# Experts' gate and up products in three fp32r passes for six of eight k-tiles, and expert weights read in whole rows per partition

## The chip, the cores and the metric

The kernel runs on one core of a Trainium2 chip. The metric is the device time of one execution in microseconds (us). Its engines: TensorE (PE), VectorE (DVE), ScalarE (ACT), GpSimd (POOL), and SyncE (SP), which issues most DMAs. 16 DMA engines move the data.

## What is computed

A two-layer decoder trunk for 512 prompt tokens and 64 sample tokens (576 rows of width 1024). Each layer is a mixer (layer 0: gated DeltaNet and pooling; layer 1: RG-LRU), a LayerNorm, a mixture of 16 experts, and a LayerNorm. The change is in the experts:

```python
    y = jnp.zeros_like(xt)
    for e in range(N_EXPERTS):
        h = jax.nn.silu(xt @ w_gate[e]) * (xt @ w_up[e])
        y = y + combine[:, e:e + 1] * (h @ w_down[e])
```

`w_gate[e]` and `w_up[e]` are 1024 x 512, `w_down[e]` is 512 x 1024, all float32: 2 MB each. Each token uses two of the 16 experts.

## The kernel before

Tokens are sorted on the chip into one block of up to 128 slots per expert. Per expert `g` (0 to 15 in layer 0, 16 to 31 in layer 1) the work is:

- POOL gathers the expert's rows of x by an indirect DMA into `XG[u]` (`u = g % 2`; weights and rows have two buffers each).
- PE transposes them in eight 128 x 128 pieces (`gather_transposed`), and DVE copies these out of PSUM into `XGT` (`x_copied`, L1985 and L1986). The eight pieces are the eight k-tiles of the contraction over 1024.
- PE multiplies `XGT` with the gate weights (`gate`, L1001) and the up weights (`up`, L1008) in plain float32. Each k-tile of 128 x 512 is one `matmul` in the source, and two MATMUL instructions in the trace.
- ACT makes the silu (L1384), DVE multiplies it with the up product (L1992), PE transposes the result (L1015), and ACT copies it out twice: rounded to fp32r as `HT_HIGH`, and in full as `HT`.
- `down` (L1026) multiplies it with the down weights in three fp32r passes: high x high, high x low, low x high. ACT makes `WDN_HIGH` by rounding, four copies of 128 x 1024; DVE subtracts that from the weights to make `WDN_LOW` (L2006), and the same for `HT_LOW` (L2005).
- ACT and DVE copy the result out (halves of `YO`), and ACT issues its store to `y_rows` (L1392).

The order on each engine is written out by hand. PE's step for expert g is `gate(g)`, `h_transposed(g-1)`, `up(g)`, `gather_transposed(g+1)`, `down(g-1)`. The last expert of a layer has its own `last_down`, plain float32 (L1037).

SP issues the weight loads in a fixed order, two experts ahead, each when its buffer has been read: after gate(g) the gate weights of g+2 (L431), after up(g) the up weights of g+2 (L434), after down(g) the down weights of g+2 (L437). As down(g-1) comes after gate(g) and up(g) on PE, and its load before theirs on SP, the three issues come together at the end of each step:

```python
                    for u in range(2):
                        sp.wait_ge(gate_ps, i * 2 + (base + u + 1))
                        sp.dma_start(WGT[u], moe_w_gate[l, bass.ds(i * 2 + (2 + u), 1)]
                                     .rearrange("o (k p) f -> p (o k) f", p=P)).then_inc(gate_in[u], 16)
                        sp.wait_ge(up_ps, i * 2 + (base + u + 1))
                        ...
                        sp.wait_ge(y0_ps, i * 2 + (base + u + 1))
```

## Time and profile before

| | |
|---|---|
| time, median of 3 runs | 1580.51 us (1578.92 to 1580.55) |
| profiled execution | 1581.12 us, of it 1578.8 us span |
| PE busy | 1350.4 us, 86% of the span |
| DVE, ACT, POOL busy | 693.1, 425.1, 208.6 us |
| mean granted PE clock | 0.903 of full speed |
| moved by DMA | 296.52 MB, mean 188 GB/s |

The rows that follow are of this one profiled execution; its time outside the span is 2.3 us. PE's busy time is modelled at a matmul's end, so that neighbouring matmuls overlap: the distance from start to start is the cost of one in a stream. The experts of layer 0 run from about 504 to 845 us, those of layer 1 from about 1190 to 1525 us.

### The profile page before, as it was taken

How to read it: one execution, taken by the hardware profiler on the slowest of the kernel's cores; microseconds unless marked ns; L12 is line 12 of the kernel's file. 1: busy time of each engine (PE TensorE's matmuls, PEld its weight loads, DVE VectorE, ACT ScalarE, POOL GpSimd, SP SyncE). 2: the span in 40 equal slices, each digit the busy share in tenths (PEclk: the TensorE clock that was granted, in tenths of full speed). 3: DMA queues.
4: the chain of work that ended last, by engine and by line, in shares of the span. 5: the costliest groups of instructions: out<-in, count | busy, mean ns of one | idle time of the engine just before them, and what ended most of it. 6: DMA issues, size and time to landing. Idle time of an engine off the chain costs nothing. (4 is left out here: it accounts for less than half of the span.)

```text
span 1578.8 us, 15547 instructions
## 1 busy us (share of the span) xinstructions
PE 1350.4 (86%) x5941; PEld 907.8 (57%) x5941; DVE 693.1 (44%) x1192; ACT 425.1 (27%) x667; POOL 208.6 (13%) x272
## 2 busy tenths in 40 slices
PE   5999878888995999999993289978959999999950
PEld 4989877854444555555551289843454555555530
DVE  2765345524244234443332823656442334333328
ACT  2533222220010222223332332262111333332213
POOL 3102142202000000000002200153001000000013
PEclk9999889995995999999996589998969999999985
DMA  6120140010616499999974511103264999999933
GB/s 182 54 81 28 54 146 1 1 48 11 216 72 226 166 363 354 368 361 357 357 267 149 188 54 54 69 39 110 80 232 147 331 358 357 355 356 357 329 118 118
DMA packets 132695, 296.52 MB, mean 188 GB/s; under 512 B 6608, under 2 KB 32937, under 8 KB 132640
## 3 DMA queue, kind: packets, MB, share of 16 engines
q1 hardware_dynamic: 120736, 252.77, 45.4%
q0 software_dynamic: 7296, 26.22, 4.7%
q10 hardware_dynamic: 4608, 16.78, 2.6%
q8 instruction: 37, 0.61, 0.2%
q14 instruction: 18, 0.15, 0.0%
HBM read 268.86 MB, written 26.89 MB: 187 GB/s over the span
## 5 line engine op out<-in xcount | busy, mean ns | idle before, releaser
L1001 PE MATMUL bank<-work 128*128 128x512 f32 x512 | 229.3, 601 | 5.5 <-DVE work L1986 5.5
L2006 DVE TENSOR_TENSOR WDN_LOW<-work,WDN_HIGH 128x1024 fp32r<-128x1024 f32 x120 | 141.4, 1220 | 201.6 <-ACT WDN_HIGH L1155 201.6
L1008 PE MATMUL bank<-work 128*128 128x512 f32 x512 | 225.0, 592 | 0.0
L1155 ACT ACTIVATE work<-bank 128x512 f32<-128x512 f32 (+4 forms) x180 | 79.4, 477 | 495.1 <-PE bank L1026 361.0
L1001 PEld LDWEIGHTS bank<-work 128*128 128x128 f32 x512 | 98.3, 193 | 118.6 <-issue 109.7
L1008 PEld LDWEIGHTS bank<-work 128*128 128x128 f32 x512 | 94.9, 190 | 108.1 <-issue 108.1
L1155 ACT ACTIVATE WDN_HIGH<-work 128x1024 fp32r<-128x1024 f32 x120 | 116.8, 1044 | 18.4 <-ACT work L1155 18.4
L1026 PE MATMUL bank<-WDN_HIGH,HT_HIGH 128*128 128x512 f32 x240 | 96.9, 404 | 0.0
L1026 PE MATMUL bank<-WDN_HIGH,HT_LOW 128*128 128x512 f32 x240 | 93.7, 390 | 0.0
L1026 PE MATMUL bank<-WDN_LOW,HT_HIGH 128*128 128x512 f32 x240 | 93.3, 389 | 0.0
L2301 POOL COPY idx_cur<-idx_all 128x1 int32 (+1 forms) x32 | 5.9, 185 | 657.4 <-PE bank L993 465.6
L927 PE MATMUL bank<-work,XT 128*128 128x512 f32 (+1 forms) x192 | 83.2, 593 | 0.0
L1155 ACT ACTIVATE W_HIGH<-work 128x1024 fp32r<-128x1024 f32 x36 | 38.0, 1058 | 150.8 <-PE bank L590 80.6
L1992 DVE TENSOR_TENSOR work<-work,bank 128x512 f32<-128x512 f32 x32 | 22.0, 688 | 114.3 <-PE bank L1008 114.3
L914 PE MATMUL bank<-work,XT 128*128 128x512 f32 x128 | 62.4, 652 | 5.6 <-POOL XT L2362 4.5
L927 PEld LDWEIGHTS bank<-work,XT 128*128 128x128 f32 (+1 forms) x192 | 32.9, 172 | 48.5 <-issue 48.5
L576 PE MATMUL bank<-ident,X 128*128 128x128 f32 (+1 forms) x120 | 18.6, 323 | 48.0 <-POOL X L2294 36.7
L1569 DVE SCALAR_TENSOR_TENSOR work<-work,par 128x512 f32<-128x512 f32 x120 | 56.9, 516 | 2.1
L1384 ACT ACTIVATE work<-bank 128x512 f32<-128x512 f32 x32 | 19.1, 597 | 136.8 <-PE bank L1001 136.8
L1330 ACT ACTIVATE lnw<-lnw 128x1 f32<-128x1 f32 (+1 forms) x20 | 4.1, 203 | 189.9 <-DVE lnw L1846 189.9
L1997 DVE COPY work<-bank 128x512 f32<-128x512 f32 x32 | 22.1, 692 | 66.2 <-PE bank L1026 46.2
L1026 PEld LDWEIGHTS bank<-WDN_HIGH,HT_LOW 128*128 128x128 f32 x240 | 45.0, 188 | 9.8
(438 smaller groups left out, 2537.1 us busy)
## 6 DMA issues: line engine op xcount, KB each, us to landing
work<-in_moe_w_gate_dram SPq DMA_DIRECT2D x32, 2048.0 KB, 14.6
work<-in_moe_w_up_dram SPq DMA_DIRECT2D x32, 2048.0 KB, 19.5
work<-in_moe_w_down_dram SPq DMA_DIRECT2D x32, 2048.0 KB, 9.9
y_rows<-work ACTq DMA_DIRECT2D x32, 512.0 KB, 8.3
work<-in_ab_w_in_dram SPq DMA_DIRECT2D x10, 1024.0 KB, 5.3
work<-in_c_w_in_dram SPq DMA_DIRECT2D x8, 1024.0 KB, 8.5
x_rows<-X SPq DMA_DIRECT2D x8, 512.0 KB, 2.6
work<-in_c_w_out_dram SPq DMA_DIRECT2D x1, 4096.0 KB, 12.7
```

The source lines that it names most:

```text
L576: last = tr(heads_of(b + k // 4, P, r)[:, k % 4, :], rows[0:r, t, P * k:P * k + P], ident[0:r, 0:r])
L914: last = mm(bank[2 * (t % 2) + half][0:ROWS[t], :], XT[:, k, tile_cols(t)], (WO_A, WO_B)[l][k][:, 512 * half:512 * half + 512], start=(k = ...
L927: last = mm(bank[2 * (t % 2) + half][0:ROWS[t], :], XT[:, k, tile_cols(t)], (WO_A, WO_B)[l][k][:, 512 * half:512 * half + 512], start=(k = ...
L1001: last = mm(bank[u][:, :], XGT[:, k, :], WGT[u][:, k, :], start=(k == 0), stop=(k == KD - 1))
L1008: last = mm(bank[2 + u][:, :], XGT[:, k, :], WUP[u][:, k, :], start=(k == 0), stop=(k == KD - 1))
L1026: last = mm(bank[7 - half][:, :], x[:, f, :], w[:, f, cols], start=(f == n == 0), stop=(f == 3 and n == 2))
L1155: return nc.scalar.activation(out, in_, ACT.Copy, scale=scale)
L1384: nc.scalar.activation(SG[u], bank[u][:, :], ACT.Silu).then_inc(sg_done, 1)
L1569: last = V.scalar_tensor_tensor(dst, src, w, dst, ALU.mult, ALU.add)
L1992: V.tensor_tensor(HB[u], SG[u], bank[2 + u][:, :], ALU.mult).then_inc(h_ready, 1)
L1997: V.tensor_copy(YO[u][:, 512:1024], bank[6][:, :]).then_inc(y1_out, 1)
L2006: last = V.tensor_tensor(WDN_LOW[u][:, f, :], WDN[u][:, f, :], WDN_HIGH[:, f, :].bitcast(F32), ALU.subtract)
```

## The change

1. Gate and up: of each weight's eight k-tiles, the first six are multiplied in three fp32r passes as `down` is, the last two stay plain float32. A unit is two k-tiles. ACT rounds a unit (a copy of 128 x 1024) into one of four `GU_HIGH` buffers, DVE subtracts it in place from the weights, and PE gives the `GU_HIGH` buffer back after its six matmuls (`gu_used`).
2. The transposed rows of x are no longer copied by DVE but rounded by ACT (three copies) and split by DVE (two subtractions). The transposed product is split straight from PSUM, so `HT` is gone.
3. `WDN_HIGH` is rounded, split and given back in four parts (`down_used`), and `down` runs over parts outside and halves inside. `last_down` is gone: the last expert is done as the others are.
4. The weights lie in SBUF as `(p k)` and not `(k p)`: a partition gets eight (or four) neighbouring rows of the matrix, 16 KB in one piece, where it had eight pieces of 2 KB (gate, up) or four of 4 KB (down). To fit, the transposes take every eighth (fourth) column (`every`).
5. Some semaphores outside the experts are shared under new numbers, and the overflow path (taken only if an expert has more than 128 tokens) follows the new layout.

```diff
             def gate(l, e, u):
-                sp.dma_start(WGT[u], moe_w_gate[l, e].rearrange("(k p) f -> p k f", p=P)).then_inc(gate_in[u], 16)
+                sp.dma_start(WGT[u], moe_w_gate[l, e].rearrange("(p k) f -> p k f", p=P)).then_inc(gate_in[u], 16)
...
-                    last = tr(heads_of(4 + k // 4)[:, k % 4, :], XG[u][:, P * k:P * k + P], ident[:, :])
+                    last = tr(heads_of(4 + k // 4)[:, k % 4, :], every(XG[u], KD, k), ident[:, :])
                 last.then_inc(xg_ps, 1)
 
+            def unit(psum, unit_no, slot_no_, n, low):
+
+                pe.wait_ge(gu_split, unit_no + 1)
+                for k in range(2 * n, 2 * n + 2):
+                    x_low = XGT_LOW_A[:, k, :] if k < 4 else XGT_LOW_B[:, k - 4, :]
+                    w_high = GU_HIGH[slot_no_][:, k % 2, :]
+                    for m, (x, w) in enumerate(((XGT_HIGH[:, k, :], w_high), (XGT_HIGH[:, k, :], low[:, k, :]), (x_low, w_high))):
+                        last = mm(psum, x, w, start=(k == m == 0), stop=(k == KD - 1 and m == 2))
+                last.then_inc(gu_used, 1)
...
+                for n in range(UNITS):
+                    unit(bank[u][:, :], 2 * UNITS * g + n, (2 * UNITS * u + n) % 4, n, WGT_LOW[u])
                 pe.wait_ge(gate_in[u], arrivals(l, pairs))
-                at_least(pe, sg_done, g - 1)
-                for k in range(KD):
-                    last = mm(bank[u][:, :], XGT[:, k, :], WGT[u][:, k, :], start=(k == 0), stop=(k == KD - 1))
-                last.then_inc(gate_ps, 1)
+                plain(bank[u][:, :], WGT[u]).then_inc(gate_ps, 1)
...
+                def round_units(which, pairs, u, g):
+
+                    w, arrived, first = (WGT, gate_in, 0) if which == "gate" else (WUP, up_in, UNITS)
+                    act.wait_ge(arrived[u], arrivals(l, pairs))
+                    for n in range(UNITS):
+                        at_least(act, gu_used, 2 * UNITS * g + (first + n - 3))
+                        copy(GU_HIGH[(2 * UNITS * u + first + n) % 4][:, :, :], w[u][:, 2 * n:2 * n + 2, :]).then_inc(gu_rounded, 1)
...
-                def step(i, v):
+                def step(i, v, more=True):
 
                     u, g = (1 + v) % 2, i * 2 + (base + 1 + v)
+                    round_units("up", i + (v + 1), u, g)
+                    h_rounded(g - 1)
                     silu(u, g)
-                    h_copied(g - 1)
+                    if more:
+                        round_units("gate", i + 2, 1 - u, g + 1)
+                        x_rounded(g + 1)
+                    round_down(i + (v + 1), u, g)
                     result(i + 1, 1 - u, g - 1, i * 2 + v)
-                    round_down(i + (v + 1), u, g)
...
                     u, g = (1 + v) % 2, i * 2 + (base + 1 + v)
+                    split_units("up", u, g)
+                    h_split(g - 1)
+                    if more:
+                        split_units("gate", 1 - u, g + 1, range(UNITS - 1))
                     h_product(u, g)
-                    x_copied(g + 1)
+                    if more:
+                        split_units("gate", 1 - u, g + 1, range(UNITS - 1, UNITS))
+                        x_split(g + 1)
+                    split_down(u, g)
                     result(i + 1, 1 - u, g - 1)
-                    split_down(u, g)
```

PE at the gate product of one expert and what follows it, before (`bank<-work` at L1001 is gate, at L1008 up, L1015 the transposes of h):

```order
L1001 MATMUL bank<-work 128x512 [waits sg_done,gate_in0,xgt_ready]
L1001 MATMUL bank<-work 128x512 x7
L1015 MATMUL bank<-ident,work 128x128 [waits y0_out,h_ready]
L1015 MATMUL bank<-ident,work 128x128 x3
L1008 MATMUL bank<-work 128x512 [waits h_ready,up_in0]
L1008 MATMUL bank<-work 128x512 x7
```

and PE of the changed kernel from the sixth k-tile of a gate product to the first matmul of the up product (L1021 is `plain`, L1043 the transposes of h):

```order
L1015 MATMUL bank<-GU_HIGH_49,XGT_HIGH 128x512
L1015 MATMUL bank<-WGT_LOW_54,XGT_HIGH 128x512
L1015 MATMUL bank<-GU_HIGH_49,XGT_LOW_B 128x512
L1021 MATMUL bank<-work 128x512 [waits gate_in1]
L1021 MATMUL bank<-work 128x512
L1043 MATMUL bank<-ident,work 128x128 [waits h_ready]
L1043 MATMUL bank<-ident,work 128x128 x3
L1015 MATMUL bank<-GU_HIGH_50,XGT_HIGH 128x512 [waits gu_split]
```

Six k-tiles have become three matmuls each; where PE waited once for a weight's load, it now waits for DVE's split of each unit.

ACT from one silu to the next step, before (`work<-bank` at L1155 is a copy of `HT`, then of the result; L1392 the store):

```order
L1384 ACTIVATE work<-bank 128x512 [waits gate_ps]
L1155 ACTIVATE HT_HIGH<-bank 128x512 [waits h_ps]
L1155 ACTIVATE work<-bank 128x512
L1155 ACTIVATE work<-bank 128x512 [waits y0_ps]
L1392 DMA y_rows<-work 128x1024 [waits y1_out,y0_out]
L1155 ACTIVATE WDN_HIGH<-work 128x1024 [waits y0_ps,down_in1]
L1155 ACTIVATE WDN_HIGH<-work 128x1024 x3
```

and the same stretch of ACT in the changed kernel (L1414 silu, L1422 the store, the last row the next step's first up unit):

```order
L1414 ACTIVATE work<-bank 128x512 [waits gate_ps]
L1173 ACTIVATE GU_HIGH_49<-work 128x1024 [waits gu_used,gate_in0]
L1173 ACTIVATE GU_HIGH_50<-work 128x1024 [waits gu_used]
L1173 ACTIVATE GU_HIGH_51<-work 128x1024 [waits gu_used]
L1173 ACTIVATE XGT_HIGH<-bank 128x512 [waits xg_ps]
L1173 ACTIVATE XGT_HIGH<-bank 128x256
L1173 ACTIVATE work<-bank 128x256
L1173 ACTIVATE WDN_HIGH<-work 128x1024 [waits down_used,down_in1]
L1173 ACTIVATE WDN_HIGH<-work 128x1024 [waits down_used] x3
L1173 ACTIVATE work<-bank 128x512 [waits down_used]
L1422 DMA y_rows<-work 128x1024 [waits y1_out,y0_out]
L1173 ACTIVATE GU_HIGH_52<-work 128x1024 [waits gu_used,up_in0]
```

Between silu and the rounding of the down weights, ACT now has the gate units of the next expert, which wait for their load, and the copies of x; the store has moved behind the rounding of the down weights, and the up units behind the store.

DVE over the same stretch in the changed kernel (L2047 splits of units, L2030 the product h, L2022 and L2023 the splits of x, L2054 those of the down weights, L2039 the copy of the result):

```order
L2047 TENSOR_TENSOR WGT_LOW_53<-work,GU_HIGH_49 128x1024 [waits gu_rounded]
L2047 TENSOR_TENSOR WGT_LOW_53<-work,GU_HIGH_50 128x1024 [waits gu_rounded]
L2030 TENSOR_TENSOR work<-work,bank 128x512 [waits sg_done,up_ps]
L2047 TENSOR_TENSOR WGT_LOW_53<-work,GU_HIGH_51 128x1024 [waits gu_rounded]
L2022 TENSOR_TENSOR XGT_LOW_A<-bank,XGT_HIGH 128x512 [waits xgt_high]
L2023 TENSOR_TENSOR XGT_LOW_B<-bank,XGT_HIGH 128x256
L2054 TENSOR_TENSOR WDN_LOW_64<-work,WDN_HIGH 128x1024 [waits down_rounded] x4
L2039 COPY work<-bank 128x512 [waits down_used]
L2047 TENSOR_TENSOR WUP_LOW_55<-work,GU_HIGH_52 128x1024 [waits gu_rounded]
```

The two gate units, the product, the third unit, x, the four down parts, the result's copy and the first up unit now stand in one row on DVE; before, the product was followed by two copies of x, the result's copy and the down splits alone.

## Rows read from the trace of the kernel before

**Rows 1.** The page's slices of the span, and its DMA queues (packets, MB, share)

```profile
DMA  6120140010616499999974511103264999999933
GB/s 182 54 81 28 54 146 1 1 48 11 216 72 226 166 363 354 368 361 357 357 267 149 188 54 54 69 39 110 80 232 147 331 358 357 355 356 357 329 118 118
...
q1 hardware_dynamic: 120736, 252.77, 45.4%
...
q8 instruction: 37, 0.61, 0.2%
```

**Rows 2.** Windows: busy us and instructions per engine, granted clock, DMA share, GB/s

```profile
680.00:720.00 40.00, 40.00 (x135) 23.13 (x134) 14.96 (x18) 12.13 (x16) 2.31 (x4) 1.00 0.99 355
```

**Rows 3.** Timeline of PE over one expert's step: start, us, line, instruction

```profile
562.04 0.39 PE L1026 MATMUL bank<-WDN_LOW,HT_HIGH 128*128 128x512 f32 x1
...
567.05 0.39 PE L1026 MATMUL bank<-WDN_HIGH,HT_LOW 128*128 128x512 f32 x1
567.28 7.03 PE L1001 MATMUL bank<-work 128*128 128x512 f32 x16
574.14 0.60 PE L1015 MATMUL bank<-ident,work 128*128 128x128 f32 x4
574.58 7.03 PE L1008 MATMUL bank<-work 128*128 128x512 f32 x16
581.45 1.04 PE L993 MATMUL bank<-ident,work 128*128 128x128 f32 x8
582.24 0.47 PE L1026 MATMUL bank<-WDN_HIGH,HT_HIGH 128*128 128x512 f32 x1
...
587.79 7.03 PE L1001 MATMUL bank<-work 128*128 128x512 f32 x16
```

**Rows 4.** Timeline of SP's issues, and the DMA view's median us to landing

```profile
567.47 0.37 SPq L437 DMA_DIRECT2D work<-in_moe_w_down_dram  x1
568.43 0.38 SPq L431 DMA_DIRECT2D work<-in_moe_w_gate_dram  x1
...
work<-in_moe_w_gate_dram SPq DMA_DIRECT2D x32, 2048.0 KB, 14.6
```

**Rows 5.** Windows within that step

```profile
568.50:583.00 14.50, 14.50 (x45) 7.29 (x44) 6.49 (x7) 5.47 (x7) 0.18 (x1) 1.00 0.99 362
571.00:572.00 1.00, 1.00 (x4) 0.38 (x2) 0.00 (x0) 1.00 (x2) 0.00 (x0) 1.00 1.01 315
575.00:576.00 1.00, 1.00 (x4) 0.51 (x3) 0.05 (x1) 0.92 (x2) 0.00 (x0) 1.00 1.02 418
579.00:580.00 1.00, 1.00 (x4) 0.45 (x3) 0.00 (x0) 0.00 (x0) 0.00 (x0) 1.00 1.05 393
```

**Rows 6.** Groups by form, 526 to 793 us: busy us, mean ns, idle before

```profile
L1155 ACT ACTIVATE WDN_HIGH<-work 128x1024 fp32r<-128x1024 f32 x48 | 46.7, 1044 | 7.7 <-ACT work L1155 7.7
...
L1997 DVE COPY work<-bank 128x512 f32<-128x512 f32 x13 | 9.0, 692 | 19.5 <-PE bank L1026 19.5
```

**Rows 7.** Timeline of DVE and ACT in that step

```profile
576.56 2.35 DVE L2006 TENSOR_TENSOR WDN_LOW<-work,WDN_HIGH 128x1024 fp32r<-128x1024 f32 x2
...
568.11 0.34 ACTq L1392 DMA_DIRECT2D y_rows<-work  x1
568.55 3.90 ACT L1155 ACTIVATE WDN_HIGH<-work 128x1024 fp32r<-128x1024 f32 x4 [0.47 <-ACT work L1155]
574.84 0.59 ACT L1155 ACTIVATE HT_HIGH<-bank 128x512 fp32r<-128x512 f32 x1
```

**Rows 8.** Timeline of PE at the start and the end of layer 0's experts

```profile
526.14 7.13 PE L1001 MATMUL bank<-work 128*128 128x512 f32 x16 [1.38 <-DVE work L1986]
...
834.02 0.63 PE L1015 MATMUL bank<-ident,work 128*128 128x128 f32 x4 [0.78 <-ACT work L1155]
835.83 8.83 PE L1037 MATMUL bank<-work 128*128 128x512 f32 x16 [1.18 <-ACT work L1155]
```

**Rows 9.** Window in the last down product

```profile
838.00:840.00 2.00, 2.00 (x4) 0.83 (x3) 0.00 (x0) 0.00 (x0) 0.00 (x0) 0.50 0.00 0
```

More of the change, by code:

```diff
@@ L46 @@
 WORK = 35340
+UNITS = 3
 class Steps:
@@ L377, in samples, with every @@
             return ap[:, TP:T].rearrange("p (s l) -> p s l", s=NS)
+        def every(rows, n, k):
+            return rows.rearrange("p (c n) -> p n c", n=n)[:, k, :]
         def at_least(engine, s, value):
@@ L996, in gate, with plain @@
+            def plain(psum, w):
+                for k in range(2 * UNITS, KD):
+                    last = mm(psum, XGT[:, k, :], w[:, k, :], start=False, stop=(k == KD - 1))
+                return last
             def gate(l, pairs, u, g):
-                pe.wait_ge(xgt_ready, g * 2 + 2)
+                pe.wait_ge(xgt_ready, g + 1)
+                at_least(pe, sg_done, g - 1)
+                for n in range(UNITS):
+                    unit(bank[u][:, :], 2 * UNITS * g + n, (2 * UNITS * u + n) % 4, n, WGT_LOW[u])
@@ L1005, in up @@
                 pe.wait_ge(up_in[u], arrivals(l, pairs))
-                at_least(pe, h_ready, g - 1)
-                for k in range(KD):
-                    last = mm(bank[2 + u][:, :], XGT[:, k, :], WUP[u][:, k, :], start=(k == 0), stop=(k == KD - 1))
-                last.then_inc(up_ps, 1)
+                plain(bank[2 + u][:, :], WUP[u]).then_inc(up_ps, 1)
             def h_transposed(u, g):
@@ L1014, in h_transposed @@
                 for f in range(4):
-                    last = tr(heads_of(7)[:, f, :], HB[u][:, P * f:P * f + P], ident[:, :])
+                    last = tr(heads_of(7)[:, f, :], every(HB[u], FF // P, f), ident[:, :])
                 last.then_inc(h_ps, 1)
             def down(l, u, g):
-                pe.wait_ge(down_split, g + (1 - l))
+                pe.wait_ge(ht_ready, g + 1)
                 at_least(pe, y1_out, g)
-                for half, done in ((1, y1_ps), (0, y0_ps)):
-                    cols = slice(512 * half, 512 * half + 512)
-                    for f in range(4):
+                for f in range(4):
+                    pe.wait_ge(down_split, 4 * g + (f + 1))
+                    for half in (1, 0):
+                        cols = slice(512 * half, 512 * half + 512)
                         for n, (x, w) in enumerate(((HT_HIGH, WDN_HIGH), (HT_HIGH, WDN_LOW[u]), (HT_LOW, WDN_HIGH))):
@@ L1027, in down @@
                                       start=(f == n == 0), stop=(f == 3 and n == 2))
[L1028 to L1039 removed]
+                    last.then_inc(down_used, 1)
             def experts(l):
@@ L1083, in overflow @@
                             for k in range(KD):
-                                last = tr(heads_of(4 + k // 4)[:, k % 4, :], XG[0][:, P * k:P * k + P], ident[:, :])
+                                last = tr(heads_of(4 + k // 4)[:, k % 4, :], every(XG[0], KD, k), ident[:, :])
                             last.then_inc(s["pe"], 1)
@@ L1094, in overflow @@
                             for f in range(4):
-                                last = tr(heads_of(7)[:, f, :], HB[0][:, P * f:P * f + P], ident[:, :])
+                                last = tr(heads_of(7)[:, f, :], every(HB[0], FF // P, f), ident[:, :])
                             last.then_inc(s["pe"], 1)
@@ L1409, in experts @@
                     step(i, 1)
-                silu(1, base + 15)
-                h_copied(base + 14)
-                result(8, 0, base + 14, 14)
-                h_copied(base + 15)
+                step(NE // 2 - 1, 0, False)
+                h_rounded(base + 15)
                 result(8, 1, base + 15, 15)
@@ L1997, in result, with split_units @@
                     V.tensor_copy(YO[u][:, 512:1024], bank[6][:, :]).then_inc(y1_out, 1)
+                def split_units(which, u, g, some=range(UNITS)):
+                    w, low, first = (WGT, WGT_LOW, 0) if which == "gate" else (WUP, WUP_LOW, UNITS)
+                    for n in some:
+                        dve.wait_ge(gu_rounded, 2 * UNITS * g + (first + n + 1))
+                        high = GU_HIGH[(2 * UNITS * u + first + n) % 4][:, :, :].bitcast(F32)
+                        V.tensor_tensor(low[u][:, 2 * n:2 * n + 2, :], w[u][:, 2 * n:2 * n + 2, :], high, ALU.subtract)\
+                            .then_inc(gu_split, 1)
@@ L2008, in split_down, with step @@
-                    last.then_inc(down_split, 1)
-                def step(i, v):
+                        dve.wait_ge(down_rounded, 4 * g + (f + 1))
+                        V.tensor_tensor(WDN_LOW[u][:, f, :], WDN[u][:, f, :], WDN_HIGH[:, f, :].bitcast(F32),
+                                        ALU.subtract).then_inc(down_split, 1)
+                def step(i, v, more=True):
                     u, g = (1 + v) % 2, i * 2 + (base + 1 + v)
+                    split_units("up", u, g)
+                    h_split(g - 1)
+                    if more:
+                        split_units("gate", 1 - u, g + 1, range(UNITS - 1))
@@ L2026, in experts @@
                     step(i, 1)
-                h_product(1, base + 15)
-                result(8, 0, base + 14)
+                step(NE // 2 - 1, 0, False)
+                h_split(base + 15)
                 result(8, 1, base + 15)
```

172 lines of the change are left out of this document (91 added, 81 removed).

## The prediction

> **What bounds the kernel now.** I read the slices of the span first. In the two experts' stages DMA stands at 9 and near 355 GB/s [rows 1]. A window of 40 us inside shows both sides full: PE busy for all 40.00 us at granted clock 1.00, DMA share 0.99 [rows 2]. Which of the two sets the pace is read from the timeline of PE: one expert takes 587.79 - 567.28 = 20.51 us, and no row of it has a wait in front [rows 3]. So PE is the bound, and DMA has almost nothing to spare: about 7.3 MB per expert (three weights of 2.10 MB, a gather and a store of 0.52 MB each) in 20.51 us is 356 GB/s. DVE and ACT are busy 14.96 and 12.13 us of 40 [rows 2].
>
> The margin of the loads matters now. All three of a step are issued together when down ends at 567.3: down at 567.47, gate at 568.43, up behind [rows 4]. The gate load lands 14.6 us later, at 583.0, which is G = 15.7 us after the end of down. Today PE wants it at 587.8, so 4.8 us are spare.
>
> **What PE saves.** Plain float32: L1001 to L1015 is 6.86 us for 16 instructions, 0.429 each, 0.858 per k-tile [rows 3]. Three passes: from 562.04 to 567.28 are 23 starts of L1026, 0.228 each, 0.683 per k-tile [rows 3]. The saving is 0.175 us on each of 12 k-tiles per expert, 2.1 us. PE alone would need 18.4 us per expert. Over 32 experts that is 67 us, if nothing else waits: 1581 - 67 = 1514.
>
> **What ACT and DVE get.** ACT gets six copies of 128 x 1024 per expert at 1.044 us [rows 6] (0.95 apart in a row, 3.90 us for four [rows 7]), and the copies of x; it had 6.2 us of work per expert (12.13 x 20.51/40) and gets about 13. DVE gets six subtractions at 1.18 (2.35 us for two [rows 7]), 7.1 us on top of 7.7, about 15. Both fit in 18.4, so neither is a bound by its sum. The order is what costs.
>
> **The chain that I expect to set the pace.** The gate load of expert k+2 is still issued only when down(k-1) has ended. PE wanted it one whole step later; ACT now wants it in the middle of the step, right behind silu, to round its units, and ACT is in order: behind that wait stand the copies of x, the four parts of the down weights, the result's copy, its store, and the next up units. On DVE nearly all of these stand in one row too. From the landing of the gate weights:
>
> - ACT rounds the first unit: 1.04
> - DVE splits two units, 2.35; product h, 0.65; third unit, 1.2
> - DVE splits x: 0.69 for 512 columns as L1997 [rows 6], and 0.35 by size for 256; 1.05
> - DVE splits four down parts, 2 x 2.35 = 4.7, and copies the result, 0.69
> - ACT issues the store it held back for that copy, 0.34 [rows 7] and 0.1 for the handover
> - ACT rounds the first up unit, 1.04; DVE splits it, 1.2
>
> Together 14.4 us; then PE can start up(k+2). From there PE needs up (18 x 0.228 + 4 x 0.429 = 5.8), the transposes (0.79 from 581.45 to 582.24) and down (5.55 to 587.79) [rows 3], 12.2 us, until down(k+1) ends, which is two steps after the end of down(k-1). So two experts take G + 14.4 + 12.2 = G + 26.6 us, or twice 18.4 if that is more. Today two take 41.0. The change gains only while G is under 14.4, or a little above with the edges below.
>
> **G after the change.** Transfers start 1.2 us after down ends (568.5 [rows 5]). Ahead of the gate weights' last byte go down, gate, the store and some of up, which ran beside: by the window 362 GB/s x 14.5 us = 5.25 MB [rows 5]. Whole rows do not occur in the trace. Bounds for their pace: the same 362 GB/s from below; from above 418, the best microsecond, when 4 KB pieces of down and the store ran together [rows 5]. Pieces of 2 KB ran at 393 and the start of down at 315 [rows 5]. I take 400, nearer the upper row, because fewer and longer pieces lose less between them, and because the slow start is of one kind of piece only. With queued whole loads less of up should run ahead; I count half, 4.98 MB. G = 1.2 + 4.98/0.400 = 13.6. The bounds are 12.5 (4.72 MB at 418) and 15.7.
>
> Two experts then take 13.6 + 26.6 = 40.2, so 20.1 per expert against 20.51: a gain of 0.4. PE would wait 3.4 us in every second step, mostly in front of up.
>
> **The transfer page.** A rule of the Trainium skill speaks against even that: HBM Reference, section Specifications (TRN2), gives about 358 GB/s as the effective bandwidth per core, though it adds that a core streaming alone measures well above. The trace's 355 GB/s over 40 us looks like that figure; its 393 and 418 in single microseconds do not. By 358, G would be 1.2 + 4.98/0.358 = 15.1, two experts 41.7, and the sum 1584 in place of 1565. A pace capped like that is the slower rival below, which is worked out from the rows alone.
>
> **The sum.** Per layer: the first step after the preloaded experts has its weights and gains the full 2.1. Some 13 steps gain 0.4 each, 5.3. Gate and up of the first expert gain 2.1, but x now goes through ACT and then DVE in both transposes that PE waits for (today 1.38 us of waiting [rows 8]; then 0.59 + 0.6 on ACT [rows 7] and 1.05 on DVE, 0.9 more each), so 0.3 is left. The last down: 24 x 0.228 = 5.5 for 16 x 0.429 = 6.9, less 1.2 because the result's copy before it stands behind the rounding of the last down part and h is split after it is rounded; 0.2. Together 7.9 per layer, 15.8 for two. Profiled time 1581.1 less 15.8 is 1565.3; the median is 0.6 below the profiled execution, so 1565.
>
> Costed at nothing: `down` by parts (same 24 matmuls); the last two k-tiles' wait for the load (landed before its units were rounded); the routing ahead of the experts, where ACT and DVE round and split the first units while the gather is under way (without that cover three splits more, 3.5 us per layer); the semaphores elsewhere. Transposes of every eighth column appear in no row: nothing from below, and from above as much again as today's 0.79 and 0.44, which on the two-step chain is 0.8 to 1.2 per two experts, 11 to 16 us in all. I take nothing, as the same 12 pieces go through PE.
>
> **Rivals.**
>
> - *The loads come in time, and PE sets the pace.* For it: PE has no other wait, and 418 GB/s exists. If the store does not run ahead of the gate weights, G = 1.2 + 4.2/0.418 = 11.2, two experts 37.8, 18.9 each: 13 x 1.6 + 2.6 = 23 per layer, 1581 - 47 = 1534. The end of this case is 1514. Against it: G would have to fall by 4 us. Chance 0.18 (1512 to 1550).
> - *No change.* At about 366 GB/s G is 14.8 and the slower steps eat the 2.6 at the edges: 1578 to 1584. For it: the long window at 362. Chance 0.12.
> - *Slower: whole rows run at the same pace, and ACT wants them earlier.* G stays 15.7, two experts take 42.3, 21.15 each, 0.64 more: 13 x 0.64 - 2.6 = 5.7 per layer, 1592. It decides from 366 GB/s down. For it: 362 over 14.5 us. A sign that long pieces may even be slow: queue q8 moved 0.61 MB in 37 pieces of 16 KB in 0.2% of 16 engines' span, 50 us, 12 GB/s per engine, while q1 moved 252.77 MB in 45.4%, 22 GB/s [rows 1]; but single pieces for another destination don't tell of a stream. At 12 GB/s per engine G would be 27 and the time about 1740. Chance 0.16.
> - *Slower: PE's clock.* Before the last down PE waits 0.78 and 1.18 us, and its 16 instructions take 8.83 us in place of 7.03 [rows 8] with a stretch at granted clock 0.50, the 1.2 GHz level [rows 9]. After 1.38 us of waiting only 0.1 was lost [rows 8]. If every wait of 3.4 us brings 1.8 us of that, 13 times, 23 us go, and 1565 becomes 1588. Against it: the waits come after full work and partly split in two. Chance 0.10.
> - *Forecast:* 1550 to 1577, 0.44.
>
> **Range and chances.** 1565. From 1538 to 1592 I leave out the best end and the slowest loads, about 2 in 10. A measurement of this kernel tells about 0.2%, 3.2 us. Faster is 0.44 + 0.18 = 0.62, the same 0.12, slower 0.26.
>
> **What the changed profile would show.** The gate and up passes 0.228 us apart; steps that alternate or lie near 20 us; waits of PE in front of the units for DVE's splits and of ACT for the gate load; gate landing near 12.5 us after issue; a DMA rate near 400 in the burst; DVE without a gap from the third unit to the up unit. I am wrong if PE has no waits (the loads land by 11 us), if the whole rows run at 362 or less, if the granted clock falls in the loop, or if the transposes' instructions are longer.

## The result, and the profile after

The changed kernel took 1591.07 us (median of 5, 1587.50 to 1592.16) beside 1580.55 for the kernel before (5, 1578.92 to 1581.03): ratio 1.0064, 95% interval 1.0049 to 1.0079. It is slower by some 10 us; forecast was a gain of 15. The profiled execution took 1592.14 us, of it 1590.4 span, 11.6 more than before. The page of the changed kernel:

```profile
PE 1309.9 (82%) x6341; PEld 1002.1 (63%) x6341; DVE 909.5 (57%) x1394; ACT 636.9 (40%) x931; POOL 224.8 (14%) x272
...
DMA packets 63068, 296.58 MB, mean 186 GB/s; under 512 B 6608, under 2 KB 32937, under 8 KB 50720
...
PE 56%; DVE 17%; DMA 14%; issue 5%; ACT 4%; POOL 1%; ACTq 0%; SPq 0%; POOLq 0%; DVEq 0%
DMA work<-in_moe_w_gate_dram 12%; PE bank L1015 8%; PE bank L1055 6%; PE bank L939 5%; PE bank L601 4%; PE bank L602 4%; PE bank L629 3%; PE bank L630 3%; PE bank L926 3%; PE bank L1021 3%; DVE WDN_LOW L2054 2%; ACT GU_HIGH L1173 2%; PE bank L1148 2%; PE bank L950 1%; DVE X L1875 1%
...
L1173 ACT ACTIVATE GU_HIGH<-work 128x1024 fp32r<-128x1024 f32 x192 | 189.9, 1050 | 219.6 <-DMA work<-in_moe_w_gate_dram 117.3
...
work<-in_moe_w_gate_dram SPq DMA_DIRECT2D x32, 2048.0 KB, 13.3
work<-in_moe_w_up_dram SPq DMA_DIRECT2D x32, 2048.0 KB, 17.8
work<-in_moe_w_down_dram SPq DMA_DIRECT2D x32, 2048.0 KB, 8.0
```

PE is busy 40 us less than before, and the kernel is 12 us longer. The chain that ended last now holds the gate load with 12%, and in front of its units ACT waited 117 us for that load. It lands 13.3 us after its issue, 14.6 before [rows 4].

SP's issues of the down loads mark the ends of PE's steps. Before, all were 20.5 us apart. After, in layer 0, they are 18.5, 23.1, 18.5, 22.8, 19.1, 23.1, 19.6, 23.0, 18.5, 22.7, 18.7, 22.4 and 18.5: the alternation of two that was forecast, with a pair at 41.6 us on average (41.5 in layer 1), where 40.2 was forecast and 41.0 stood before. One pair (one of the longer, 42.2 us), in the timelines of SP, ACT, DVE and PE; in brackets what ended a wait:

```profile
631.08 0.33 SPq L449 DMA_DIRECT2D work<-in_moe_w_down_dram  x1
631.60 0.49 SPq L443 DMA_DIRECT2D work<-in_moe_w_gate_dram  x1
...
673.27 0.33 SPq L449 DMA_DIRECT2D work<-in_moe_w_down_dram  x1
...
646.15 2.96 ACT L1173 ACTIVATE GU_HIGH<-work 128x1024 fp32r<-128x1024 f32 x3 [6.92 <-DMA work<-in_moe_w_gate_dram]
...
657.62 0.34 ACTq L1422 DMA_DIRECT2D y_rows<-work  x1
658.42 2.96 ACT L1173 ACTIVATE GU_HIGH<-work 128x1024 fp32r<-128x1024 f32 x3 [4.02 <-PE bank L1015]
...
647.25 2.36 DVE L2047 TENSOR_TENSOR WGT_LOW<-work,GU_HIGH 128x1024 fp32r<-128x1024 f32 x2 [6.75 <-ACT GU_HIGH L1173]
...
652.19 4.62 DVE L2054 TENSOR_TENSOR WDN_LOW<-work,WDN_HIGH 128x1024 fp32r<-128x1024 f32 x4
656.72 0.69 DVE L2039 COPY work<-bank 128x512 f32<-128x512 f32 x1
659.51 3.50 DVE L2047 TENSOR_TENSOR WUP_LOW<-work,GU_HIGH 128x1024 fp32r<-128x1024 f32 x3 [2.10 <-ACT GU_HIGH L1173]
...
652.42 0.79 PE L1015 MATMUL bank<-GU_HIGH,XGT_HIGH 128*128 128x512 f32 x1 [2.30 <-DVE XGT_LOW_B L2023]
...
660.78 0.50 PE L1015 MATMUL bank<-GU_HIGH,XGT_HIGH 128*128 128x512 f32 x1 [0.31 <-DVE WUP_LOW L2047]
```

Down ended at 630.9, and ACT has the gate weights at 646.15: G = 15.3. From there DVE has no gap until it copies the result; PE starts up at 660.78, 14.6 us after the landing, and the next but one down ends 12.3 us later. (ACT's wait at 658.42 is put down to PE, but the store ahead of it on ACT had waited for DVE's copy.) The same stretches in windows (columns as in [rows 2]):

```profile
632.10:646.10 14.00, 13.64 (x59) 10.00 (x58) 6.64 (x7) 4.45 (x7) 0.45 (x2) 1.00 0.99 387
640.00:642.00 2.00, 2.00 (x11) 1.65 (x10) 0.49 (x1) 0.00 (x0) 0.00 (x0) 1.00 1.06 446
...
652.00:655.00 3.00, 2.58 (x6) 2.10 (x7) 3.00 (x4) 2.40 (x4) 0.00 (x0) 0.53 0.88 344
680.00:720.00 40.00, 37.20 (x153) 28.48 (x154) 28.00 (x30) 23.45 (x32) 4.19 (x4) 0.96 0.85 335
```

The burst moved at 387 GB/s, 5.42 MB before the gate weights' last byte. After its wait of 2.30 us PE ran at granted clock 0.53, near the 1.2 GHz level. In this pair that lies beside DVE's chain: PE still reached up 0.31 us before the split was ready (660.78). It is not so in every pair. The up product of 701.83 starts after a wait of 1.79 us for its split, and eight of its matmuls then start 0.42 us apart with nothing of DVE's left beside them: down ends 13.9 us after the start of up in place of 12.3. That is a pair of 42.7 us. In 40 us PE stands still for 2.8, and DMA's share is 0.85 where it was 0.99.

The rest of the loss is outside the steps. The timelines of POOL before and after, where a layer's first rows are fetched (first the kernel before, then the changed one):

```profile
498.65 0.19 POOL L2301 COPY idx_cur<-idx_all 128x1 int32<-128x1 int32 x1 [102.02 <-DVE idx_all L1978]
499.89 1.08 POOL L2303 DMA_INDIRECT work<-x_rows,idx_cur  x1 [1.05 <-issue]
```

```profile
498.53 1.02 POOL L2358 COPY idx_cur<-idx_all 128x1 int32<-128x1 int32 x1 [102.03 <-DVE idx_all L2015]
500.60 2.12 POOL L2360 DMA_INDIRECT work<-x_rows,idx_cur  x1 [1.05 <-issue]
...
498.29 3.49 DVE L2047 TENSOR_TENSOR WGT_LOW<-work,GU_HIGH 128x1024 fp32r<-128x1024 f32 x3
...
505.96 1.95 PE L1005 MATMUL bank<-ident,work 128*128 128x128 f32 x8 [7.80 <-DMA work<-x_rows,idx_cur]
510.20 0.79 PE L1015 MATMUL bank<-GU_HIGH,XGT_HIGH 128*128 128x512 f32 x1 [2.29 <-DVE XGT_LOW_B L2023]
...
818.33 0.50 PE L1015 MATMUL bank<-GU_HIGH,XGT_HIGH 128*128 128x512 f32 x1 [1.74 <-DVE XGT_LOW_B L2023]
...
826.67 0.47 PE L1015 MATMUL bank<-GU_HIGH,XGT_HIGH 128*128 128x512 f32 x1 [1.79 <-DVE WUP_LOW L2047]
...
839.93 0.72 PE L1043 MATMUL bank<-ident,work 128*128 128x128 f32 x4 [1.72 <-ACT work L1173]
843.02 0.56 PE L1055 MATMUL bank<-WDN_HIGH,HT_HIGH 128*128 128x512 f32 x1 [2.37 <-DVE HT_LOW L2034]
```

Beside DVE's splits POOL's copy of the indices takes 1.02 us and its indirect DMA 2.12, and the rows land later by 1.8 us (505.96 for 504.18). The copy and the first split end together, near 499.5. At the end of the layer PE waits 1.74, 1.79 and 2.37 us for splits and 1.72 for ACT's copy of the result, where two waits of 0.78 and 1.18 stood before [rows 8]. Layer by layer, in us of the profiled executions, with what was forecast:

| stretch | forecast | layer 0 | layer 1 |
|---|---|---|---|
| until the first rows have landed | 0 | +1.8 | +1.4 |
| from there to the first down issue | -2.4 | -0.5 | 0.0 |
| 13 steps | -5.3 | +1.7 | +0.8 |
| last down issue to the end of the last down | -0.2 | +2.7 | +2.8 |

Before rounding they add up to 10.6; 1.0 more lies in the mixer and behind the experts.

### The profile page after: what moved, and what is told of

It reads as the page before. It is cut to its first block, busy times and chain, and to the rows that moved or that the text cites. A ratio compares the mean times of both kernels' runs of the same rounds, so it can differ in the third digit from the quotient of the medians.

```text
span 1590.4 us, 17518 instructions
## 1 busy us (share of the span) xinstructions
PE 1309.9 (82%) x6341; PEld 1002.1 (63%) x6341; DVE 909.5 (57%) x1394; ACT 636.9 (40%) x931; POOL 224.8 (14%) x272
## 3 DMA queue, kind: packets, MB, share of 16 engines
q1 hardware_dynamic: 51104, 252.77, 41.5%
## 4 chain that ended last, share of the span: by engine, by line
PE 56%; DVE 17%; DMA 14%; issue 5%; ACT 4%; POOL 1%; ACTq 0%; SPq 0%; POOLq 0%; DVEq 0%
DMA work<-in_moe_w_gate_dram 12%; PE bank L1015 8%; PE bank L1055 6%; PE bank L939 5%; PE bank L601 4%; PE bank L602 4%; PE bank L629 3%; PE bank L630 3%; PE bank L926 3%; PE bank L1021 3%; DVE WDN_LOW L2054 2%; ACT GU_HIGH L1173 2%; PE bank L1148 2%; PE bank L950 1%; DVE X L1875 1%
## 5 line engine op out<-in xcount | busy, mean ns | idle before, releaser
L1173 ACT ACTIVATE GU_HIGH<-work 128x1024 fp32r<-128x1024 f32 x192 | 189.9, 1050 | 219.6 <-DMA work<-in_moe_w_gate_dram 117.3
L1015 PE MATMUL bank<-GU_HIGH,XGT_HIGH 128*128 128x512 f32 x384 | 164.6, 429 | 49.8 <-DVE XGT_LOW_B L2023 36.4
L2047 DVE TENSOR_TENSOR WGT_LOW<-work,GU_HIGH 128x1024 fp32r<-128x1024 f32 x96 | 114.4, 1221 | 124.7 <-ACT GU_HIGH L1173 124.7
L2054 DVE TENSOR_TENSOR WDN_LOW<-work,WDN_HIGH 128x1024 fp32r<-128x1024 f32 x128 | 150.6, 1222 | 8.3 <-ACT WDN_HIGH L1173 4.9
L2047 DVE TENSOR_TENSOR WUP_LOW<-work,GU_HIGH 128x1024 fp32r<-128x1024 f32 x96 | 112.2, 1221 | 61.1 <-ACT GU_HIGH L1173 61.1
L1015 PEld LDWEIGHTS bank<-GU_HIGH,XGT_HIGH 128*128 128x128 f32 x384 | 77.5, 202 | 76.2 <-issue 32.9
L1021 PE MATMUL bank<-work 128*128 128x512 f32 x256 | 120.1, 591 | 0.0
L1015 PE MATMUL bank<-GU_HIGH,XGT_LOW_A 128*128 128x512 f32 x256 | 108.5, 424 | 0.0
L1015 PE MATMUL bank<-WGT_LOW,XGT_HIGH 128*128 128x512 f32 x192 | 83.2, 433 | 0.0
L1015 PE MATMUL bank<-WUP_LOW,XGT_HIGH 128*128 128x512 f32 x192 | 75.6, 394 | 0.0
L1021 PEld LDWEIGHTS bank<-work 128*128 128x128 f32 x256 | 48.2, 188 | 35.9 <-issue 30.8
## 6 DMA issues: line engine op xcount, KB each, us to landing
work<-in_moe_w_gate_dram SPq DMA_DIRECT2D x32, 2048.0 KB, 13.3
work<-in_moe_w_up_dram SPq DMA_DIRECT2D x32, 2048.0 KB, 17.8
```

Source lines behind the costliest of these rows:

```text
L1015: last = mm(psum, x, w, start=(k == m == 0), stop=(k == KD - 1 and m == 2))
L1021: last = mm(psum, XGT[:, k, :], w[:, k, :], start=False, stop=(k == KD - 1))
L1173: return nc.scalar.activation(out, in_, ACT.Copy, scale=scale)
L2047: V.tensor_tensor(low[u][:, 2 * n:2 * n + 2, :], w[u][:, 2 * n:2 * n + 2, :], high, ALU.subtract)\
L2054: V.tensor_tensor(WDN_LOW[u][:, f, :], WDN[u][:, f, :], WDN_HIGH[:, f, :].bitcast(F32), ALU.subtract).then_inc(down_split, 1)
```

## The experiments

Ratios are to the kernel before, measured beside each run. "The reordered kernel" is the changed one with sp_order's edit.

**Loads issued earlier (sp_order).** SP walks one expert ahead: gate and up of g+3 go out before it waits for down(g).

```diff
+                sp.wait_ge(gate_ps, base + 1)
+                gate(l, 2, 0)
+                sp.wait_ge(up_ps, base + 1)
+                up(l, 2, 0)
-                with sp.Fori(0, NE // 2 - 1) as i:
+                with sp.Fori(0, NE // 2 - 2) as i:
                     for u in range(2):
-                        sp.wait_ge(gate_ps, i * 2 + (base + u + 1))
-                        sp.dma_start(WGT[u], moe_w_gate[l, bass.ds(i * 2 + (2 + u), 1)]
+                        sp.wait_ge(gate_ps, i * 2 + (base + u + 2))
+                        sp.dma_start(WGT[1 - u], moe_w_gate[l, bass.ds(i * 2 + (3 + u), 1)]
...
```

> The changed kernel, with one edit: SP issues the gate and up loads of expert g+3 as soon as gate(g+1) and up(g+1) are done, ahead of the wait for down(g), so the three loads no longer come in one burst after down. Theory 1 (the late gate load G sets the pace, 15.1 + 14.6 + 12.4 us per two experts): ACT's waits for the gate load (117 us in all) go, PE's waits before the gate units go, one expert takes 18.4 to 18.9 us, and the time falls from 1591 by 26 x 2.1 to about 1535 (1525 to 1550). Theory 2 (DVE's and ACT's own row of work sets the pace): the waits only move, one expert stays above 20 us, 1580 to 1591. Theory 3 (the DMA engines cannot carry 7.3 MB per 18.5 us): share 1.00, about 19.5 us per expert, 1555.

1531.3 us, ratio 0.9688 (0.9676 to 0.9701). A window, the DMA view and SP's issues in this kernel:

```profile
680.00:720.00 40.00, 39.94 (x173) 30.59 (x172) 30.93 (x32) 25.67 (x34) 3.63 (x4) 1.00 0.99 389
...
work<-in_moe_w_gate_dram SPq DMA_DIRECT2D x32, 2048.0 KB, 9.8
...
628.86 0.33 SPq L447 DMA_DIRECT2D work<-in_moe_w_gate_dram  x1
...
641.34 0.33 SPq L453 DMA_DIRECT2D work<-in_moe_w_down_dram  x1
```

PE waits for nothing, steps are 18.3 and 18.9 us, and the gate load lands 9.8 us after an issue that is itself 12.5 us ahead of the end of down (628.86 and 641.34). So the late issue of gate and up is the cause of the slower pairs; which of the two loads it is, gate_early tells below. ACT and DVE, at 25.7 and 30.9 of 40 us, keep up.

**The same order without the change (before_sp_order)**, the same edit in the kernel before.

> The kernel before with the same edit of SP's order alone. Theory 1: no change within 0.2% (1580.5), because PE never waited for a load there. If it gains more than 5 us, the loads did cost the kernel before something that no row of waits showed.

1580.76 us, 1.0001 (0.9992 to 1.0010). The order alone is worth nothing: PE was the bound and no load was late.

**Whole rows alone (before_rows).** The kernel before with `(p k)` loads and the `every` transposes.

```diff
-                                     .rearrange("o (k p) f -> p (o k) f", p=P)).then_inc(gate_in[u], 16)
+                                     .rearrange("o (p k) f -> p (o k) f", p=P)).then_inc(gate_in[u], 16)
...
-                    last = tr(heads_of(4 + k // 4)[:, k % 4, :], XG[u][:, P * k:P * k + P], ident[:, :])
+                    last = tr(heads_of(4 + k // 4)[:, k % 4, :], every(XG[u], KD, k), ident[:, :])
```

> The kernel before with the layout alone: weights in whole rows of 16 KB per partition, transposes of every eighth and every fourth column. If strided transposes cost nothing: 1580.5 within 0.2%, same starts on PE, loads landing 1 to 2 us sooner (down 8, gate 13 us). If they cost as much again, 0.79 + 0.44 us per expert: 32 x 1.2 = 39 us more, 1620. If a third of that: 1593.

1580.55 us beside 1580.19, 1.0001 (0.9992 to 1.0010); one of the eleven executions took 3576 us, which nothing here explains, the others 1579.99 to 1582.97. The gate load lands in 13.2 us, hidden. Steps take 20.57 us in place of 20.51; on PE's timeline the transposes account for 0.04 of the 0.06 (0.80 and 0.47 us from their start to the next product's, for 0.79 and 0.44). That is some 2 us in the whole kernel by the steps, which the medians can't tell from nothing. My upper bound of 11 to 16 us is out.

**PE kept busy through its wait (busy_wait).** Ten matmuls into the gate bank, overwritten by the product, ahead of the wait for x. They are work that the result doesn't need. A layer's first two experts go without them; all others get them, also in the steps in which PE did not wait.

```diff
-            def gate(l, pairs, u, g):
+            def gate(l, pairs, u, g, fill=True):
+                at_least(pe, sg_done, g - 1)
+                for _ in range(10 if fill else 0):
+                    mm(bank[u][:, :], HT_HIGH[:, 0, :], HT_HIGH[:, :, :].rearrange("p f c -> p (f c)"), start=True, stop=True)
                 pe.wait_ge(xgt_ready, g + 1)
-                at_least(pe, sg_done, g - 1)
```

> The changed kernel with ten more fp32r matmuls of 512 columns (2.3 us of PE, their result is overwritten) between down and the next gate, ahead of PE's wait for the split of x, so that PE works where it waited. They leave the kernel's results alone. Theory 1 (the granted clock falls after that wait, but the 1.4 us lost lie beside DVE's splits, which end last before up): the clock stays at 1.00 in the loop, and the time stays within 5 us of 1591. Theory 2 (the fall of the clock is on the path, some 1.4 us per two experts): 13 x 1.4 = 18 us less, 1573. If PE's own time mattered in every step the ten matmuls would add up to 30 x 2.3 = 69 us.

1592.62 us, 1.0076 (1.0061 to 1.0091). In the loop the granted clock is 1.00 and PE is busy for all 40 us of a window:

```profile
680.00:720.00 40.00, 40.00 (x177) 31.31 (x177) 26.99 (x29) 22.21 (x31) 2.82 (x4) 1.00 0.89 352
```

The steps are 20.7 to 21.0 us, and 13 take 270.2. The time is that of the changed kernel, but the run can't decide between its two theories. The ten matmuls (10 x 0.228 = 2.3 us) come in both steps of a pair, so PE alone now needs 18.4 + 2.3 = 20.7 us per step and 41.5 per pair, which is what the changed kernel's pairs take with their waits. The 1573 us of theory 2 could not have come out. What the half clock costs in the changed kernel is read from its own trace instead. In 20 of its pairs ACT's wait for the gate load shows, and there up starts 14.3 us or more after the landing, as DVE's chain of 14.4 asks. Down ends 12.3 us after the start of up in 19 of the 20, so there was no half clock behind up; in the one from 701.83 it ends 13.9 us after. So where it delays the end of down, the half clock costs some 1.6 us, in one of the 20.

**Old layout in the changed kernel (old_rows).** The rearrangements and transposes of before_rows, the other way round.

> The changed kernel with the weights in their former layout (pieces of 2 and 4 KB, transposes of neighbouring columns). Theory 1 (the landing of the gate load, G, sets the pace): G goes from 15.1 back to 15.7 us or a little over, two experts take 42.7 in place of 42.1, 8 us more in all: about 1599, and gate lands 14.6 us after issue in place of 13.3. If the layout didn't matter: 1591. If the transposes of every eighth column cost: under 1591.

1609.67 us, 1.0191 (1.0177 to 1.0205): 19 us over the changed kernel, 10 more than expected. Down, gate and up land after 8.9, 14.4 and 21.0 us, pairs take 42.4 to 43.5. So the whole rows did give something, in this kernel: without them the first half of the change costs 29 us. Landing explains 1.1 us per pair, 13 to 14 us in all. The two profiled executions differ by 14.2 us (1606.30 and 1592.14) and their steps by 14.5, so the profiles hold no more than that; the rest of the 19 is spread between executions (1606.30 to 1612.41) and was not taken apart.

**The result's copy ahead of the down splits (result_early).**

```diff
                         x_rounded(g + 1)
-                    round_down(i + (v + 1), u, g)
                     result(i + 1, 1 - u, g - 1, i * 2 + v)
+                    round_down(i + (v + 1), u, g)
...
-                    split_down(u, g)
                     result(i + 1, 1 - u, g - 1)
+                    split_down(u, g)
```

> The changed kernel with the copy of the result moved ahead of the down weights' rounding (ACT) and splits (DVE), as it stood before. ACT's store and the rounding of the first up unit then run beside DVE's four down splits, which takes some 1.7 us out of the 14.6 from the gate load's landing to up. Theory 1 with the clock: PE's own path then ends last (gate starts 6.3 us after the landing and takes 5.8 + 0.6 + 1.4 us lost to the clock, 14.1), so only 0.5 us per two experts are gained: 1585. Theory 2 (the clock costs nothing anywhere): the full 1.7, 13 times, 22 us: 1569.

1608.83 us, 1.0182 (1.0168 to 1.0196): a miss, in sign too. ACT's timeline shows why:

```profile
654.19 0.60 ACT L1173 ACTIVATE work<-bank 128x512 f32<-128x512 f32 x1 [2.90 <-PE bank L1055]
655.10 0.34 ACTq L1422 DMA_DIRECT2D y_rows<-work  x1
655.57 3.90 ACT L1173 ACTIVATE WDN_HIGH<-work 128x1024 fp32r<-128x1024 f32 x4 [0.78 <-DVE work L2039]
```

The result exists only when PE's down has ended. ACT now stands 2.9 us in front of it, with the down rounding and the next up units behind, and PE waits some 2.1 us for up's first split in every step and no longer in every second. The place I had called the costly one, behind four splits, was the one where the copy never had to wait for PE.

**Both (early_busy).** result_early with the ten matmuls.

> As result_early, and with the ten matmuls ahead of the next gate that keep PE busy where it waited. Theory 1 with the clock: without the clock's fall PE reaches up 12.7 us after the landing, DVE's split of the first up unit is ready at 12.9, so 1.7 us per two experts are gained over the changed kernel: about 1569, some 16 us under result_early. Theory 2 (the clock costs nothing): the same as result_early.

1599.18 us, 1.0125 (1.0109 to 1.0140): a miss against 1569 as well, but 9.7 us under result_early. The 1569 was out of reach, for the reason given under busy_wait: with ten matmuls in every step PE alone needs 20.7 us. Steps are 20.7 to 21.0, without the 22.4 that occurred there. In result_early the half clock (the 1.2 GHz level) follows four of the 13 waits of some 2 us in layer 0 (behind the one that ends at 704.18, eight matmuls start 0.42 us apart), and a step with it takes 22.4 us in place of 20.8. So with no slack beside DVE it costs 1.6 us in such a step, and the six steps of 22.4 or 22.5 us in the two layers make up the 9.7.

**The reordered kernel with the old layout (sp_order_old_rows).**

> SP's order as in sp_order, and the weights in their former layout. Seven tenths of the bytes of a step then go in 2 and 4 KB pieces: at the rate of the long windows with them, 362 to 387 GB/s, 7.34 MB take 19.0 to 20.3 us, more than PE's 18.4. Theory A (whole rows are what lets DMA keep up): 1545 to 1575, DMA share 1.00, PE waiting for loads again. Theory B (the layout doesn't matter once the loads are issued in time): 1531.

1530.06 us, 0.9682 (0.9669 to 0.9696), level with sp_order. With each load issued when its buffer is free, pieces of 2 and 4 KB are as good: the window 680 to 720 shows

```profile
680.00:720.00 40.00, 39.90 (x172) 30.05 (x171) 30.44 (x32) 26.01 (x33) 3.64 (x4) 1.00 1.04 397
```

397 GB/s, in the layout whose 355 [rows 2] I had read as near DMA's end. The 355 was PE's pace, 7.3 MB per step of 20.5 us; a DMA share of 0.99 did not mean that nothing was to spare.

**Only gate early (gate_early).** As sp_order, with up left in the burst behind down.

```diff
-                        sp.wait_ge(up_ps, i * 2 + (base + u + 2))
-                        sp.dma_start(WUP[1 - u], moe_w_up[l, bass.ds(i * 2 + (3 + u), 1)]
...
                         sp.wait_ge(down_used, i * 8 + 4 * (base + u + 1))
                         sp.dma_start(WDN[u], moe_w_down[l, bass.ds(i * 2 + (2 + u), 1)]
...
+                        sp.wait_ge(up_ps, i * 2 + (base + u + 2))
+                        sp.dma_start(WUP[1 - u], moe_w_up[l, bass.ds(i * 2 + (3 + u), 1)]
```

> The changed kernel, but SP issues only the gate load early: the gate weights of expert g+3 go out when gate(g+1) is done, ahead of the wait for down(g). Down and up still go out together at the end of each down, down first. Theory 1 (the late landing of the gate load alone turns the step; up was never late): ACT finds its gate weights there, PE has no waits in the loop, steps are 18.3 to 18.9 us, up lands some 12 us after its issue, well ahead of its use 25 us later, and the time is 1531 to 1534 us. Theory 2 (what helped in the reordered kernel was that the up load left the burst as well, so that the burst is short and DMA never idles): the burst still holds 4.2 MB and DMA is idle in part of a step; a step stays near 19.5 to 20 us and the time is 1545 to 1565 us.

1532.12 us, 0.9696 (0.9683 to 0.9710), steps as in sp_order, no wait of PE in the loop. The gate load alone was late.

**The burst in another order (burst_gate_first).** As sp_order, but all three issued behind the wait for down(g), gate first.

```diff
-                        sp.wait_ge(gate_ps, i * 2 + (base + u + 2))
+                        sp.wait_ge(down_used, i * 8 + 4 * (base + u + 1))
...
-                        sp.wait_ge(up_ps, i * 2 + (base + u + 2))
...
-                        sp.wait_ge(down_used, i * 8 + 4 * (base + u + 1))
```

> The changed kernel, but within the burst at the end of down(k-1) SP issues gate(k+2), up(k+2), down(k+1) and not down(k+1), gate(k+2), up(k+2). Nothing is issued earlier than in the changed kernel. Theory 1 (chain behind the landing of what ACT asks for): the gate weights land near 1.2 + (2.1 + 0.5) MB / 0.40 = 8 us after the end of down and are in time; down(k+1) now lands last, 1.2 + 6.8/0.40 = 18 us after, and ACT asks for it some 14 to 15 us after. From there down's rounding 1.04, four splits 4.7, the result's copy 0.7, the store 0.44, the first up unit 1.04 and 1.2, so up starts 27 us after the burst, and 12.3 us more give 39.3 per two experts, in place of the 41.7 of the changed kernel: 13 x 1.2 x 2 = 31 us less, about 1560 us. Theory 2 (the issue time of the whole burst sets the pace, not its order): the time stays within 3 us of the changed kernel's 1591.

1597.35 us, 1.0103 (1.0087 to 1.0119). Neither: not the 1560 of the chain, and 6 us over the changed kernel. Its DMA view, and one pair on ACT and PE:

```profile
work<-in_moe_w_gate_dram SPq DMA_DIRECT2D x32, 2048.0 KB, 7.9
work<-in_moe_w_up_dram SPq DMA_DIRECT2D x32, 2048.0 KB, 13.3
work<-in_moe_w_down_dram SPq DMA_DIRECT2D x32, 2048.0 KB, 17.7
...
656.30 3.90 ACT L1183 ACTIVATE WDN_HIGH<-work 128x1024 fp32r<-128x1024 f32 x4 [4.71 <-DMA work<-in_moe_w_down_dram]
...
665.99 0.79 PE L1025 MATMUL bank<-GU_HIGH,XGT_HIGH 128*128 128x512 f32 x1 [3.85 <-DVE WUP_LOW L2057]
666.58 0.63 PE L1025 MATMUL bank<-WUP_LOW,XGT_HIGH 128*128 128x512 f32 x1
667.01 0.63 PE L1025 MATMUL bank<-GU_HIGH,XGT_LOW_A 128*128 128x512 f32 x1
```

The lateness went from gate to down, as expected, and its terms were 18.9 (18 expected) and 9.7 (9.0). What I had left out stands in the last rows: PE now has one wait of 3.9 us in place of 2.3 and 0.3, and behind it 14 matmuls start 0.43 us apart and not 0.228. That is 2.8 us in this pair, in the up product, with no slack beside it: 15.1 us to the end of down, not 12.3. This pair takes 43.9. Behind the other waits of layer 0, of 3.3 to 4.5 us, 6 to 11 matmuls were slow.

**The first gather undisturbed (gather_first)**, on the reordered kernel: DVE's first splits wait for POOL's second copy of indices.

```diff
-                    G.tensor_copy(idx_cur[:, u:u + 1], idx_all[:, 0, bass.ds(e, 1)])
+                    taken = G.tensor_copy(idx_cur[:, u:u + 1], idx_all[:, 0, bass.ds(e, 1)])
+                    if isinstance(e, int):
+                        taken.then_inc(consts_ready, 1)
...
+                dve.wait_ge(consts_ready, 1 + 2 * (l + 1))
                 split_units("gate", 0, base)
```

> The reordered kernel (gate and up issued ahead of the wait for down), and in addition DVE holds its splits of a layer's first gate units back until POOL has copied the indices of the second gather. Theory 1: in the changed kernel these splits run beside POOL's first index copy and indirect DMA, which take 1.02 and 2.12 us in layer 0 where they took 0.19 and 1.08 before the change, so that the first rows land 1.8 us later in layer 0 and 1.4 us later in layer 1; held back, the splits are done before the rows have landed and been rounded, and the kernel takes 3.2 us less than the reordered kernel of the same call. POOL's copy shows 0.19 and its indirect DMA 1.08 again. Theory 2: POOL's longer records are something else (the new placement of the buffers), and the copy stays at 1 us; the time is that of the reordered kernel within 1 us or some tenths longer.

and beside it the reordered kernel again (sp_order_again):

> The reordered kernel once more, as the base for the run with the held back splits in the same call. Expected: 1531.3 us as measured before, within 0.7 us.

1527.42 us (1525.66 to 1531.47), 0.9667 (0.9654 to 0.9680), beside 1530.98 (1530.43 to 1531.68), 0.9692 (0.9678 to 0.9705). The medians differ by 3.6 us, as expected by 3.2, though the ranges overlap. The mechanism is plain in the rows of gather_first:

```profile
501.19 0.19 POOL L2371 COPY idx_cur<-idx_all 128x1 int32<-128x1 int32 x1 [102.05 <-DVE idx_all L2027]
502.44 1.07 POOL L2375 DMA_INDIRECT work<-x_rows,idx_cur  x1 [1.07 <-issue]
...
506.75 1.94 PE L1017 MATMUL bank<-ident,work 128*128 128x128 f32 x8 [5.94 <-DMA work<-x_rows,idx_cur]
```

POOL's copy is at 0.19 us again, and PE's wait for the rows at 5.94 in place of 7.82 (7.11 in place of 8.24 in layer 1), 3.0 us in both layers. Longer records from the buffers' new placement are ruled out. The time is less certain than the mechanism: the intervals of the two ratios overlap slightly, and the execution that was profiled took 1531.47 us, as its routing ahead of layer 0's experts was already done 3.0 us later (DVE's last step of it at 500.85 and not 497.87). By the medians this is the best version, 3.3% under the kernel before.

## Why the prediction was wrong

**Right.** PE was the bound, and the passes are 0.228 us apart: PE alone needs 18.4 us per expert, and where loads are in time steps are 18.3 and 18.9. ACT and DVE fit. The gate load, asked for earlier by ACT and issued no earlier, sets a chain of two steps that alternate. The chain behind the landing was 14.6 us for 14.4, and the product and down behind it 12.3 for 12.2. Strided transposes at nothing were right to 0.04 us per step.

**Step that failed, 1: "G after the change", 13.6.** It is 15.3 in the pair shown, by the mean pair of 41.6 less 26.9 it is 14.7, and read from ACT's waits in 20 pairs it is 13.5 to 16.2, 14.6 on average. In the pair shown the pace was 387 GB/s and not 400, and 5.42 MB and not 4.98 went ahead of the gate's last byte: 0.70 MB of them are up's, where I had counted half of the 0.53 that ran beside before. So 13 steps gave +1.7 and +0.8 us in place of -5.3 each: 13 us of the 27 that the profiled sum is off. Both errors lie inside the bounds I gave (12.5 to 15.7), but the sign of the whole change hung on them: the case decides at G = 14.4, and I took a middle value and gave 0.62 to a gain. My reason for 400, that fewer and longer pieces lose less between them, holds at most for the burst (the gate load lands 1.1 us earlier than in old_rows); spread out, whole rows moved at 389 to 397 GB/s and the old pieces at 390 to 398.

**Step that failed, 2: the edges, -2.6 per layer.** They were +4.0 and +4.2, another 13 us. I costed the preparation at nothing since ACT and DVE do it while the gather is under way; but DVE's splits stand in the way of POOL, which issues that gather: 1.8 and 1.4 us. The Trainium skill (SBUF — State Buffer, section SBUF: two separate sides) says that a DVE instruction with two SBUF inputs and a GpSimd one that reads SBUF share a port pair, that whichever starts first has it for the whole instruction, and that the other one blocks. The trace agrees: the copy of 0.19 us takes 1.02 beside a split of 1.2 that started 0.24 us ahead of it, and 0.19 again when the splits are held back. PE's wait for x before the first two gates is 2.29 us, as I worked out (1.38 + 0.9). Behind the first the half clock was there before too (9.52 us for the 7.03 of a gate product); behind the second it is new, eight matmuls 0.42 us apart, some 1.6 us, and was not in the sum. At the end of the layer I looked only at the last down and forecast a gain of 0.2; the four waits there are 7.6 us in all for 2.0 before. The last two of them, behind the result's copy and its store on ACT and DVE, were not tried in another order.

**The rivals.** The measured time, 1591, is that of "whole rows run at the same pace, and ACT wants them earlier" (1592), but only half for its reason: its steps would have been 21.15 and were 20.8, since whole rows did land sooner, and the edges made up the rest. The clock rival had a condition that didn't hold, half clock on the path in every pair: in the changed kernel's loop it is there in one pair of the 20 read, 1.6 us (its trace; busy_wait could not show it), and it costs more where the slack beside DVE is gone (burst_gate_first, result_early). "The loads come in time" gave 1534; made true by sp_order it measures 1531. The rule of the Trainium skill that I weighed (HBM Reference, section Specifications (TRN2)), about 358 GB/s per core, gave 1584, nearer than my 1565, but that is luck: 387 GB/s moved in the burst, and 389 to 397 over 40 us when loads were spread. The trace agrees with what that section adds, that a core streaming alone measures well above. My own reading that DMA had almost nothing to spare was wrong for the same reason: 355 GB/s was what PE's steps asked for.

## What to carry to other kernels

When a change makes an engine ask for a load earlier in its step, move the issue of the load by as much, or the faster engine only waits: here another order of SP's issues made -3.1% out of +0.6%, and was worth nothing before the change. A shared issue point is worse than its order: whichever load goes last is late, and one long wait can cost PE's clock as well. A filler that keeps an engine busy through its waits must stand only where it waits, or it sets the pace itself and the run decides nothing. Cost the edges of a loop by their own rows, POOL's queue included, since in a near balance they decide the sign.
